# Three waits reordered in a two-block transformer kernel: attention exponentials, level masks and a norm's mean

## What is computed

```python
# first block: attention and a gated MLP, then a gated addition ("PLE")
gate = sigmoid(rms_norm(h, ln_ple) @ w_ple_gate)
h = h + (p @ w_ple_proj) * gate
# second block, layers l = 0 and 1
x = x + (ab_mixer if l == 0 else c_mixer)(rmsnorm(x, mix_norm[l]))
x = x + mem_cross_attn(rmsnorm(x, xa_norm[l]), memn)      # 4 heads of 256
x = x + square(relu(rmsnorm(x, mlp_norm[l]) @ w1)) @ w2
# inside c_mixer: gated delta net, chunks of 64, 8 heads
sol = triangular_solve(lower + eye, rhs, unit_diagonal=True)
# inside mem_cross_attn
p = softmax((q @ k.T) * 256 ** -0.5);  o = p @ v
```

## Time and profile before

| what | value |
|---|---|
| median of the runs | 1328.74 us |
| the profiled execution's own time | 1329.45 us |
| its span, first to last instruction | 1327.6 us |
| PE busy | 1271.8 us (96%) |
| DVE busy, ACT busy, POOL busy | 792.4, 707.6, 128.3 us |
| granted TensorE clock, mean | 0.985 of full |
| DMA | 205.52 MB, mean 155 GB/s |

### The profile page before, as it was taken

How to read it: one execution, slowest core, us unless ns; L and a number is a source line. 1 busy time by engine, 2 the same in 40 slices (tenths; PEclk the granted TensorE clock), 3 DMA queues, 4 the chain that set the end, 5 groups by cost and what they waited for, 6 DMA issues and landing times.

```text
span 1327.6 us, 22040 instructions
## 1 busy us (share of the span) xinstructions
PE 1271.8 (96%) x9160; PEld 1152.9 (87%) x9160; DVE 792.4 (60%) x1163; ACT 707.6 (53%) x1118; POOL 128.3 (10%) x146
## 2 busy tenths in 40 slices
PE   6999999999999989999999999998999999999997
PEld 6988899998888877888999888987998888999886
DVE  5786678885456555645555446786645635655444
ACT  6767666664476534644655335554355634655433
POOL 6000001110000000000111000105600000111000
PEclk9999999999999998999999999998999999999999
DMA  9433465555544523543555555532203534465550
GB/s 335 161 117 107 143 191 187 176 180 196 188 138 175 190 69 137 175 143 112 169 182 189 191 177 159 183 120 92 92 8 111 190 128 139 149 189 190 191 191 32
DMA packets 141430, 205.52 MB, mean 155 GB/s; under 512 B 3730, under 2 KB 118802, under 8 KB 141330
## 3 DMA queue, kind: packets, MB, share of 16 engines
q1 hardware_dynamic: 141330, 204.11, 46.5%
HBM read 203.05 MB, written 1.05 MB: 154 GB/s over the span
## 4 chain that ended last, share of the span: by engine, by line
PE 84%; DVE 7%; ACT 5%; issue 2%; POOL 1%; DMA 1%; SPq 0%; DVEq 0%; ACTq 0%; POOLq 0%
PE ps L303 40%; PE ps L365 27%; PE ps L383 5%; PE ps L2080 2%; DVE weights_lo L282 2%; PE ps L1705 1%; ACT weights_hi L279 1%; PE ps L2142 1%; PE ps L1727 1%; PE ps L487 1%; POOL arena L2368 1%; DVE split_arena L518 1%; ACT normed L904 1%; DMA weights<-in_w_in 1%; PE ps L755 0%
## 5 line engine op out<-in xcount | busy, mean ns | idle before, releaser
L282 DVE TENSOR_TENSOR weights_lo<-weights,weights_hi 128x1024 fp32r<-128x1024 f32 x379 | 471.4, 1255 | 253.5 <-ACT weights_hi L279 251.3
L303 PE MATMUL ps<-split_arena,weights_hi 128*128 128x256 f32 x3056 | 561.8, 286 | 8.5 <-DVE split_arena L518 6.8
L279 ACT ACTIVATE weights_hi<-weights 128x1024 fp32r<-128x1024 f32 x379 | 396.7, 1056 | 274.3 <-PE ps L365 182.7
L303 PEld LDWEIGHTS ps<-split_arena,weights_hi 128*128 128x128 f32 x3056 | 479.3, 193 | 17.2 <-issue 12.0
L303 PE MATMUL ps<-split_arena,weights_lo 128*128 128x256 f32 x1528 | 433.4, 284 | 0.0
L303 PEld LDWEIGHTS ps<-split_arena,weights_lo 128*128 128x128 f32 x1528 | 294.4, 193 | 0.0
L365 PE MATMUL ps<-weights_hi,split_arena 128*128 128x512 f32 x992 | 272.7, 392 | 2.4 <-ACTq L1877 1.6
L365 PEld LDWEIGHTS ps<-weights_hi,split_arena 128*128 128x128 f32 x992 | 184.5, 188 | 41.7 <-issue 2.9
L365 PE MATMUL ps<-weights_lo,split_arena 128*128 128x512 f32 x496 | 153.7, 390 | 0.0
L365 PEld LDWEIGHTS ps<-weights_lo,split_arena 128*128 128x128 f32 x496 | 93.1, 188 | 19.7
L1885 POOL TENSOR_TENSOR normed<-normed 128x512 f32<-128x512 f32 x32 | 34.1, 1065 | 502.0 <-ACTq L1877 502.0
(11 more groups left out here) (364 smaller groups left out, 1321.3 us busy)
## 6 DMA issues: line engine op xcount, KB each, us to landing
weights<-in_mlp_w SPq DMA_DIRECT2D x64, 1024.0 KB, 5.3
weights<-in_w_up SPq DMA_DIRECT2D x22, 1024.0 KB, 5.1
weights<-in_c_w_in SPq DMA_DIRECT2D x16, 1024.0 KB, 5.4
weights<-in_w_in SPq DMA_DIRECT2D x14, 1024.0 KB, 6.3
weights<-in_ab_w_in SPq DMA_DIRECT2D x12, 1024.0 KB, 5.3
weights<-in_w_down SPq DMA_DIRECT2D x11, 1024.0 KB, 4.9
weights<-in_xa_wv SPq DMA_DIRECT2D x8, 1024.0 KB, 4.9
weights<-in_xa_wq SPq DMA_DIRECT2D x8, 1024.0 KB, 5.2
```

What stands on the lines that cost most here:

```text
L279: act.activation(h, r, ACT.Copy).then_inc(s_hi, 1)
L282: dve.tensor_tensor(l, r, h.bitcast(F32), ALU.subtract).then_inc(s_lo, 1)
L303: mm = pe.matmul(o, w[:, k, :], x[:, k, :], start=(k == 0 and i == 0), stop=(k == DC - 1 and i == 2))
```

## The change

It does three things. In `xa_act` the exponentials of head 0 go ahead of the copy of query unit 2, with one split that DVE needs for them kept ahead. In `c_pool` level 0 is masked for both groups first, and PE waits for `c_lt` at 2 and not 3. In the norm behind the PLE addition the mean of token tile 0 moves out of `ple_dve` to behind DVE's two splits.

```diff
@@ ple_dve
                 dve.tensor_tensor(x, x, PG[:, b % 2, :], ALU.add).then_inc(s_x, 1)
-                if b == 1:
-                    first_half_dve(4, 0)
@@ xa_act
             query(0)
+            split(act, first_part[first_unit[f"xq{l}"] + 2] + 2)
+            exps(0)
             query(2)
-            exps(0)
             turned_p(0)
@@ c_pe
-            pe.wait_ge(named("c_lt"), 3)
+            pe.wait_ge(named("c_lt"), 2)
             pe.wait_ge(named("c_prep"), 2)
@@ c_pool
-            for hg in range(2):
-                pool.wait_ge(named("c_prep"), 2 * hg + 2)
-                masked(0, hg)
-                masked(1, hg)
+            for lvl in range(2):
+                for hg in range(2):
+                    if lvl == 0:
+                        pool.wait_ge(named("c_prep"), 2 * hg + 2)
+                    masked(lvl, hg)
@@ vector block
             ple_dve()
             split_through(dve, "ple_gate", 4)
+            first_half_dve(4, 0)
             norm_dve(4, X)
```

## The result

| | kernel before | changed kernel |
|---|---|---|
| median of 4 runs each on one chip | 1329.33 us (1327.57 to 1330.22) | 1312.11 us (1310.81 to 1312.72) |
| profiled execution: own time | 1329.45 us | 1312.71 us |
| its span | 1327.6 us | 1311.0 us |

What follows compares the result with a forecast made beforehand. TensorE was taken as the bound, gaining only where it stood idle: 8.4 + 3.9 + 2.4 = 14.7 us off 1329.45 gives 1314.75, and with the median 0.7 lower 1314.0 us; forecast 1312.8 to 1316.3 (chance 0.57), range 1310.5 to 1319.

Steps and rivals of the forecast that it cites:

- rival 1: At the solve: first mask gets in ahead of DVE's split (+1.0) or clock returns earlier; 1311 to 1313 us, chance 0.18.
- What bounds the kernel: TensorE (PE) is the bound nearly everywhere; reordering another engine pays only at PE's idle gaps, four in all.
- Cross attention, 8.4 us: Both layers: earlier exponentials remove PE's 2.52 us wait and scores run at full clock; 4.1 plus 4.3 us gained.
- The norm's mean, 3.9 us: Behind the PLE addition: low splits come earlier, key piece runs without wait in 2.9 us; gain 3.9 us.
- The masks, 2.4 us: Start of the solve: both group 1 masks run beside a DVE split, PE starts 2.4 us earlier.
- Level 1's slack: Solve: level 1's masks done about 923.9, PE asks at 925.5; no cost if PE gains under about 4 us.
- The clock: Solve: remaining 3.4 us gap still lowers the clock, so nothing is given back; at most some 4.0 us if all returned.
- Rival 3: Weight transfers set the pace, so each saved microsecond is waited for later; 1328.7 us, no change, chance 0.04.
- Rival 4: Cross attention: exponentials hold unit 3's high splits behind a late minimum; 1331.5 us, slower, chance 0.03.

Runs made afterwards that it cites:

- Five dummy matmuls: Kernel before plus five matmuls on unread data behind query unit 2 in each layer, filling PE's gap; 1327.49 us beside 1329.43.
- the splits away: Changed kernel with DVE's two low splits moved behind the solve's first round; 1311.70 us beside 1312.87 for the changed kernel, on another chip 1311.19 beside 1312.62.
- masks alone: Kernel before with only the level 0 masks of both groups put first and PE waiting for count 2; 1327.06 us beside 1329.25.
- mean-only kernel: Kernel before with only the norm's mean behind the PLE addition moved behind DVE's two low splits; 1324.56 us beside 1329.25.
- cross attention alone: Kernel before with only head 0's exponentials moved ahead of the copy of query unit 2, both layers; 1321.5 us beside 1329.25.

## Why the prediction was right, step by step

The measured 1312.1 us is inside the range, but below the forecast's own 1312.8 to 1316.3: it is the outcome that rival 1 (1311 to 1313, chance 0.18) described, mainly by the first of its two ways. All three terms were too small, by 0.2, 0.7 and 1.1 us. The sum of 14.7 should have been 16.7.

**What bounds the kernel.** Right. The four gaps of PE gave 16.7 us where the spans differ by 16.6. That the two agree so well is luck: unedited stretches moved by +1.7, -1.4 and -0.4 us.

**Cross attention, 8.4 us.** Measured 4.2 + 4.4 = 8.6, in the changed kernel and alone. Five dummy matmuls divide it: 5.5 us of waiting and 3.1 of clock, where the clock fell. In the medians the term alone was 7.75: the clock's share, and that of the stretches without an edit, varies from execution to execution. ACT's moved splits cost nothing, as said.

**The norm's mean, 3.9 us.** The mechanism held row by row (take 0.4 off the times of the trace after): the splits end at 397.98, so at 397.6 (predicted 397.7), the mean comes at 397.89, so at 397.5, and the key piece has no wait and takes 2.9 us. It measured 4.6. The step that was mis-sized is the norm behind it: "the scaled half ... ends at 402.0", with "0.3" kept for the later first logarithm. It ended at 401.10 + 0.72 = 401.82, so at 401.4 by the times of the trace before. The second logarithm had come at 400.53, so at 400.1, where 400.7 was foretold. The first logarithm was 0.35 us later than before and not 0.6 (398.13 - 0.41 against 397.37), and behind it ACT lost its wait of 0.39 us for the residual, as foretold, and some 0.2 us more. PE's 16 transposes took 2.02 us in all, without the wait of 0.4 that I allowed.

```profile
400.95 2.02 PE L487 MATMUL ps<-ident,normed 128*128 128x128 f32 x16
```

**The masks, 2.4 us.** The step that failed is "because DVE's split starts at 914.12, a little ahead of 914.2". The 914.2 has a hop of 0.2 us for POOL in it. In the run the mask started 0.13 us after the product's end (904.53 + 0.69 = 905.22) and the split 0.14: the first mask took 1.28 us, as if alone, and PE waited 2.39 us for round 0 where 3.4 was foretold. That was the first half of rival 1, at +1.0, and it came: 3.5 us. The order hangs on 0.01 us, and POOL's mask before it had ended only 0.15 us ahead of the start (the idle time in its row), so foreseeing it would have taken luck; yet it was the same in all six traces that have the new order and the splits. Here the Trainium skill (SBUF — State Buffer, "Who interferes with whom") fits: it has a DVE instruction with two SBUF inputs and a reading GpSimd instruction shut each other out, the first to issue holding the port. The trace agrees: 1.28 us for the mask that issued first and 2.15 for the next, and with the splits away 7.92 us for six. Which of the two issues first only the run could show, and that order, by 0.01 us, was worth about 0.9 us (2.15 - 1.28). (The 918.9 in the prediction should be 914.12 + 2 x (1.2 + 1.29) = 919.1, and the 2.2 beside it 2.0; nothing else used them.)

**Level 1's slack, "as long as PE gains less than about 4 us".** Right by the letter, with nothing to spare. PE gained 3.4 us at round 0 and 0.5 more up to round 1, and waited 0.26 (0.52 and 0.40 in the other two traces); where the clock did not fall (masks alone) it waited 2.45.

**The clock.** "The gap is now 3.4 us, still longer than the two of 2.52 us that lowered it" rested on two samples. The gap became 2.39 and lowered the clock partly (0.68, then 0.50) in the changed kernel, not at all in the masks-only kernel, and one of 2.52 did not lower it in the mean-only kernel. As a rule of the form "a gap this long lowers the clock" the step is refuted; the price of the fall in cross attention was right. At the solve "I give nothing back here" came true by luck. Without their waits rounds 0 and 1 were 0.9 us shorter than before, since the clock stood low for less of them, and PE's new waits (0.26 us at round 1, 0.34 at round 2, 0.15 more at round 3) took nearly all of it.

**The rest of 14.7 against 17.2 us.** The medians of the single edits give 7.75 + 4.7 + 2.2 = 14.6 us, and all together 17.2, 17.5 and 17.6 in three comparisons. The traces, one of each kernel, place most of the rest. From the sums of squares to the end of the solve the masks alone gain 137.10 - 134.54 = 2.6 us and in the changed kernel 3.5 (133.56; 133.27 and 133.39 in the other two traces), because alone PE waits longer at round 1, and the slow clock comes behind that wait. And the trace of cross attention alone loses 1.2 us in the key piece, at the gap that the norm's edit closes; its instructions up to there are those of the kernel before, so this is a difference between executions and no cost of the edit. These two make 2.1 us of 2.6 to 3.0. What is left lies in unedited stretches that differ by up to 2 us in both directions. That the mixer differs by the clock is shown by its rows; why an execution gets the one length or the other isn't settled by any run here.

**The other rivals.** Rival 3 (transfers) fell: no stretch grew by what an earlier one gained. Rival 4 (slower) needed a minimum 14 us late; it came 0.04 us ahead of the exponentials, and even two more splits ahead of them cost 0.38 us a layer.

## What to carry to other kernels

Look for the few places where the bounding engine stands idle, follow the wait to its last releaser, and ask whether that releaser's input had been ready long before: an instruction whose input is ready belongs ahead of a copy or a sum that still waits. Price such a gap as its length plus the slow matmuls in its wake, but treat the second part as something that may or may not come, and check what the next count behind the gap needs, since a round that starts earlier also asks earlier for the next level. Keep split instructions with two SBUF inputs on DVE away from a mask on POOL that PE waits for (0.88 us a mask here). And before a small difference far from the edit is explained, compare traces of kernels that are the same up to there.

## What the runs showed of the chip that I had not expected

- The same instructions with the same waits have more than one length. A gap of 2.52 us was followed by eight scores in 2.71 us or in 1.73; the `ab` mixer took 138.0 to 140.0 us, the norm ahead of `c` 36.35 to 38.34 and the start up to the first of the three key pieces 391.3 to 393.7 in fourteen traces; 24 matmuls behind a gap of 2.96 us took 4.62 or 5.49. One trace of each kernel can thus show a gain or loss of 1 to 2 us far from the edit that is none of its doing.
- Half the clock was seen in the wake of a gap as short as 2.39 us (0.68, then 0.50), and a mean of 0.92 in a stretch whose gap is 1.19 us.
- POOL's mask started 0.13 us after the end of DVE's product that it waits for, and DVE's own next instruction 0.14 us after it. Two engines went on 0.01 us apart, and which was first was worth about 0.9 us.
